# Three up tiles of a feed-forward layer as float32 matmuls ahead of two layer norms

## The reference, cut to what matters

```python
mod = jax.nn.silu(c) @ w_ada[l] + b_ada[l]
sh1, sc1, g1, sh2, sc2, g2 = jnp.split(mod, N_MOD, axis=-1)
...
x = layer_norm(ALPHA * x + g1[:, None] * mix, ln1_g[l], ln1_b[l])

h = layer_norm(x) * (1.0 + sc2[:, None]) + sh2[:, None]
up = causal_dwconv(h @ w_up[l], w_dw_f[l], b_dw_f[l])
v, gt = jnp.split(up, 2, axis=-1)
f = (jax.nn.gelu(gt) * v) @ w_down[l]
x = layer_norm(ALPHA * x + g2[:, None] * f, ln2_g[l], ln2_b[l])
```

## Time and profile before

| what | value |
|---|---|
| median of 3 runs | 1081.65 us (1080.99 to 1084.04) |
| the profiled execution's own time | 1080.48 us |
| its span in the trace | 1078.7 us |
| PE busy | 1042.5 us (97%), 7724 matmuls |
| DVE busy | 775.7 us (72%) |
| ACT busy | 601.7 us (56%) |
| chain that ended last | PE 80%, DVE 12%, ACT 5%, issue 2%, DMA 1% |
| mean granted TensorE clock | 0.992 |

### The profile page before, as it was taken

The page is one execution under the profiler, slowest core; times in us unless marked ns, Lnnn a source line. Parts: engine busy times, 40 slices in busy tenths (PEclk is TensorE's granted clock), DMA queues, the critical chain, the costliest instruction groups (busy, mean ns, idle before and its releaser), DMA issues.

```text
span 1078.7 us, 18838 instructions
## 1 busy us (share of the span) xinstructions
PE 1042.5 (97%) x7724; PEld 982.2 (91%) x7724; DVE 775.7 (72%) x1327; ACT 601.7 (56%) x1029; POOL 1.3 (0%) x13
## 2 busy tenths in 40 slices
PE   7999998999999989989999999999999999999997
PEld 7999998999999988889987899999899878999996
DVE  7989998799877777776667655555789766555555
ACT  5577555666555577552555545544555655545543
POOL 0000000000000000000000000000000000000000
PEclk9999999999999999999999999999999999999999
DMA  9995564477766533441323566566465436565511
GB/s 375 419 363 196 180 237 173 156 251 272 243 194 194 177 98 98 130 145 60 98 79 118 195 196 193 179 194 192 141 212 165 132 116 236 180 191 193 179 60 39
DMA packets 58021, 195.47 MB, mean 181 GB/s; under 512 B 10320, under 2 KB 10704, under 8 KB 57680
## 3 DMA queue, kind: packets, MB, share of 16 engines
q1 hardware_dynamic: 56784, 194.21, 53.5%
q10 hardware_dynamic: 1152, 0.07, 0.1%
HBM read 192.94 MB, written 1.31 MB: 180 GB/s over the span
## 4 chain that ended last, share of the span: by engine, by line
PE 80%; DVE 12%; ACT 5%; issue 2%; DMA 1%; ACTq 0%; POOL 0%; DVEq 0%; POOLq 0%; SPq 0%
PE ps L551 71%; PE ps L848 3%; DVE lo L1740 2%; PE ps L634 2%; DVE B L2152 1%; ACT hi L1158 1%; DVE raw L1727 1%; DVE sm L1917 1%; PE ps L727 1%; DVE xa L1751 0%; DVE B L1808 0%; ACT B L1529 0%; PE ps L707 0%; PE ps L753 0%; ACT L1165 0%
## 5 line engine op out<-in xcount | busy, mean ns | idle before, releaser
L1740 DVE TENSOR_TENSOR lo<-raw,hi 128x1024 fp32r<-128x1024 f32 x311 | 377.7, 1222 | 130.4 <-ACT hi L1158 129.8
L551 PE MATMUL ps<-hh,hi 128*128 128x256 f32 x1568 | 444.2, 283 | 6.8 <-DVE hl L1785 3.2
L551 PE MATMUL ps<-hl,hi 128*128 128x256 f32 x1568 | 439.4, 280 | 0.0
L551 PE MATMUL ps<-hh,lo 128*128 128x256 f32 x1568 | 439.2, 280 | 0.0
L1158 ACT ACTIVATE hi<-raw 128x1024 fp32r<-128x1024 f32 x311 | 324.8, 1052 | 51.0 <-PE ps L551 45.4
L551 PEld LDWEIGHTS ps<-hh,hi 128*128 128x128 f32 x1568 | 296.5, 189 | 10.8 <-DVE lo L1740 3.4
L551 PEld LDWEIGHTS ps<-hl,hi 128*128 128x128 f32 x1568 | 296.5, 189 | 1.6
L551 PEld LDWEIGHTS ps<-hh,lo 128*128 128x128 f32 x1568 | 296.4, 189 | 0.0
L551 PE MATMUL ps<-hi,fh 128*128 128x512 f32 x192 | 76.3, 397 | 0.0
L551 PE MATMUL ps<-lo,fh 128*128 128x512 f32 x192 | 75.9, 395 | 0.0
L551 PE MATMUL ps<-hi,fl 128*128 128x512 f32 x192 | 75.8, 395 | 0.0
(11 more groups left out here) (283 smaller groups left out, 1263.0 us busy)
## 6 DMA issues: line engine op xcount, KB each, us to landing
raw<-in_w SPq DMA_DIRECT2D x359, 512.0 KB, 4.3
B<-in_t SPq DMA_DIRECT2D x2, 512.0 KB, 4.5
xa<-in_x SPq DMA_DIRECT2D x1, 1024.0 KB, 10.1
B<-in_r SPq DMA_DIRECT2D x1, 1024.0 KB, 7.8
out<-h SPq DMA_DIRECT2D x4, 256.0 KB, 2.0
cst<-in_c SPq DMA_DIRECT2D x1, 864.0 KB, 8.4
vec<-in_v SPq DMA_DIRECT2D x1, 328.5 KB, 6.4
ev<-between SPq DMA_DIRECT2D x1, 128.0 KB, 1.9
```

What stands on the lines that cost most here:

```text
L551: m = g.matmul(o, l, r, start=first and n == 0, stop=last and n == 2, skip_group_check=True)
L1740: g.tensor_tensor(lo[:, j % SPLIT, :], raw[:, PLACE[j] % RAW, :], hi[:, j % SPLIT, :].bitcast(F), ALU.subtract).then_inc(*up("lo", j))
```

## The change

The up tiles 0, 22 and 1 (`PLAIN`) are no longer taken from the normalised `h`. They are linear in it, and both norms scale and shift whole tokens. So each tile is taken as eight float32 matmuls of the raw weights with `rx`, the residual ahead of both norms times `ln1_g * (1 + sc2)`, and four more columns are carried behind the 256 tokens (`ln1_g * (1+sc2)`, `ln1_b * (1+sc2)`, `1+sc2`, `sh2`), so that the same matmul gives the four sums of columns that the means and shifts need. Later one matmul with 4 rows (`plain_mend`) adds these sums times four numbers of each token, and DVE multiplies by the token's combined scale, read from a row `rs_row`.

What each engine has more or less:

- PE: no `first_tiles` (72 fp32r matmuls of 256 columns) and no `spin` in the two norms (26); instead 24 float32 matmuls of 260 columns, three small transposes (`plain_sums`), two matmuls and two transposes for the tokens' numbers (`token_rows`), three matmuls of 4 rows (`plain_mend`).
- ACT: no `high` for three units; new are two copies of 8 columns, eight copies into `rx`, some of 2 and 4 columns, a root of 2 columns, three of 4x128, and `tokT` and `rs_row`.
- DVE: no `low` for three units; new are two products of 8 columns, three tiny ones on the tokens' numbers, and three products of 128x256 (`plain_mend`). Both late `ada` rows move ahead of the residual, and two `low` calls move in their place into the norms.
- The convolution of tiles 0, 22 and 1 reads `plain_up` in SBUF, and the banks of PSUM are shared out anew.
- `turn_in` waits for pieces in pairs.

Cut to its core:

```diff
-ROWS_AT = {**{i: 1 for i in range(20, 39)}, 26: 0, 27: 2, 28: 3, 30: 0, 31: 0, 32: 5, 35: 0, 44: 2}
+ROWS_AT = {**{i: 1 for i in range(20, 39)}, 26: 0, 27: 2, 28: 3, 30: 0, 31: 0, 32: 5, 35: 0, 39: 1, 40: 1}
...
+PLAIN = [("up", 0), ("up", FF), ("up", 1)]
+UNITS = [u for u in PLAN if u[0] != "ada" and u not in PLAIN]
...
+            def plain(t, *ks):
+                i = PLAN.index(PLAIN[t])
+                s.wait_ge(*landed(i))
+                s.wait_ge(*at("res", ("x1", 2 * t + 1)))
+                for k in ks:
+                    s.wait_ge(*at("rx", k))
+                    m = g.matmul(bank[UP_BANKS[t]][:, 0:260], raw[:, i % RAW, k * P:k * P + P], rx[:, k, 0:260], start=k == 0,
+                                 stop=k == 7, skip_group_check=True)
...
             turn_in("x1", lambda k: at("res", ("x1", k)))
-            spin(14, 6)
+            plain(0, *range(8))
             turn_out("x1")
-            turn_in("h2", lambda k: at("n_v" if k in X1_V else "n_a", ("x1", k)))
-            spin(12, 6)
-            turn_out("h2")
+            plain(1, 0)
+            turn_in("h2", lambda k: at("n_v" if k in X1_V else "n_a", ("x1", k)),
+                    lambda k: plain(1, 1 + k // 2) if k in (1, 3) else None)
+            plain_sums(0)
+            plain(1, *range(3, 8))
+            plain(2, 0, 1)
+            turn_out("h2", lambda: plain(2, 2))
+            plain_sums(1)
+            plain(2, *range(3, 8))
+            token_rows()
+            plain_mend(0)
+            plain_mend(1)
...
-                first_tiles([(kup, 0), (kup, FF), (kup, 1)], R3, h_of, [free0])
...
+                        if t == 3:
+                            plain_sums(2)
+                            plain_mend(2)
...
+            for k in range(8):
+                s.wait_ge(*at("res", ("x1", k)))
+                s.wait_ge(*at("col_sh"))
+                g.activation(rx[:, k, 0:S], xa[:, k, :], ACT.Copy, scale=rx[:, k, 256:257]).then_inc(*up("rx", k))
             normed("x1")
...
+            plain_sums(0)
+            plain_rows(0)
             normed("h2")
+            plain_sums(1)
+            plain_rows(1)
...
+            def token_rows():
+                s.wait_ge(*at("tokT_mm"))
+                g.activation(tokT, bank[4][0:4, S:2 * S], ACT.Copy).then_inc(*up("tokT"))
+                g.activation(rs_row, bank[4][:, 0:S], ACT.Copy).then_inc(*up("rs_row"))
+
+            turned_high("h2", modcol("sc2"), modcol("sh2"), h, token_rows)
+            plain_sums(2)
+            plain_rows(2)
...
-            for k in range(7):
+            for k in range(5):
                 low(UNIT["out", k] + AHEAD)
...
-            ada(late)
+            low(UNIT["out", 5] + AHEAD)
             normed("h2")
-            ada(late + 1)
+            token_scalars()
+            low(UNIT["out", 6] + AHEAD)
             turned_parts("h2", modcol("sc2"), modcol("sh2"), h)
+            plain_mend(0)
+            plain_mend(1)
             low(UNIT["out", 7] + AHEAD)
```

More of the change, by code:

```diff
@@ L699, in turn_in, with turn_out @@
                         m.then_inc(*up("tok_in", (nid, k // 4)))
-            def turn_out(nid):
+                    if between:
+                        between(k)
+            def turn_out(nid, between=None):
                 for half in range(2):
@@ L706, in turn_out @@
                         for k in range(4 * half, 4 * half + 4):
+                            if k > 5 and nid == "h2":
+                                s.wait_ge(*at("norm_a", (nid, 1)))
                             m = g.transpose(turned_out(nid, k)[:, c * P:c * P + P], nt[:, c, k * P:k * P + P], ident)
+                        if between and not half and not c:
+                            between()
                     m.then_inc(*up("turned", (nid, half)))
+            def plain(t, *ks):
[6 more added lines that the diff above has]
+                                 stop=k == 7, skip_group_check=True)
+                if k == 7:
+                    m.then_inc(*up("plain", t))
@@ new lines, in plain_sums, with plain_mend @@
+            def plain_sums(t):
+                s.wait_ge(*at("wcol", t))
+                g.matmul(bank[UP_BANKS[t]][0:4, 264:392], wcol[:, t, :], ident, is_transpose=True, start=False, stop=True,
+                         skip_group_check=True).then_inc(*up("wrow_mm", t))
+            def plain_mend(t):
+                s.wait_ge(*at("wrow", t))
+                s.wait_ge(*at("tokT"))
+                g.matmul(bank[UP_BANKS[t]][:, 0:S], wrow[:, t, :], tokT, start=False, stop=True,
+                         skip_group_check=True).then_inc(*up("mended", t))
@@ new lines, in token_rows @@
+            def token_rows():
+                s.wait_ge(*at("n_v", ("h2", 1)))
+                s.wait_ge(*at("tok4"))
+                for c in range(2):
+                    m = g.matmul(bank[4][:, c * P:c * P + P], rs_both[:, c, :].to_broadcast([P, P]), ident, start=c == 0,
+                                 stop=True, skip_group_check=True)
+                for c in range(2):
+                    m = g.matmul(bank[4][0:4, S + c * P:S + c * P + P], tok4[:, c, :], ident, is_transpose=True, start=False,
+                                 stop=True, skip_group_check=True)
+                m.then_inc(*up("tokT_mm"))
@@ L1296, in affine, with turned_high @@
                 g.activation(o[:, k, :], turned_out(nid, k), ACT.Identity, scale=gain(k), bias=bias(k)).then_inc(*up("n_a", (nid, k)))
-            def turned_high(nid, gain, bias, o):
+            def turned_high(nid, gain, bias, o, between=None):
                 def high_part(k):
```

105 lines of the change are left out of this document (79 added, 26 removed).

## The result

Over 22 runs of each, the changed kernel takes 1083.64 us (median; 1082.46 to 1086.55) and the kernel before 1080.87 (1077.63 to 1085.65). The ratio is 1.0029, with a 95% interval of 1.0020 to 1.0038: slower by some 3 us, where 1081.2 and "no change" were forecast. The spans of the profiled executions are 1081.1 and 1078.7. A second series, ten runs of the changed kernel against 27 of the one before, gave 1082.28 against 1080.93, ratio 1.0011 (0.9999 to 1.0022): 1.2 to 1.4 us, and an interval that just reaches no change. The loss is real in the first series, small in both, and its size is known only as 1 to 3 us. Kernels of different series are best compared by their ratios to the kernel before, whose median was 1080.56 to 1080.93 in the series of the experiments.

The account below looks back on a forecast made before the run. PE, busy for 97% of the span, was taken as the bound. Tile 2 starting 0.95 us early less a 0.5 us stall gave 0.45 us gained on the median 1081.65: 1081.2 us, range 1078.3 to 1083.6.

Parts of the forecast that it names:

- Out stage: Ahead of the norms: about 0.6 us more DVE work against a 0.47 us pause; cost nothing.
- first norm: Plain tile 0 fills PE's pause and keeps the clock full; turned result 1.35 us early, root not held up by rx.
- weighed rule on a drain: ACT table switch costs 1283 ns plus a drain of about 1380 ns; weighed, but not used in the sum.
- rival 3: A table load holds ACT twice as long where work stands right behind it: 1083.5 us, chance 0.03.
- Second norm: DVE's second statistics lead by 0.7 us, but the lead isn't passed on; ACT starts gain and bias as before.
- rival 2: ACT and DVE take over PE's lead in the second norm, clock full as well: 1078.25 us, chance 0.1.
- Tokens and mending: Behind the second norm PE waits 3.5 us for tokT, one low stretch adds 1.7; tile 2 starts 0.95 us early.
- The start of the sum: Base of the forecast: profiled execution of 1080.48 us and median of 1081.65, from which 0.45 us gain was taken.
- Behind it: After tile 2 starts: one stall of 0.5 us, at low of tile 25; f_lo 0 is in time.
- Rival 1: Clock stays full through the wait for tokT: gain 2.15 us, 1079.5 us, chance 0.2.
- Rival 4: PE pauses 1.7 us or more before 181, low clock with plain matmuls ahead of transposes: 1083.6 us, chance 0.1.
- Rival 5: The wait for tokT eats all that three tiles save; with 1 us more on ACT 1082.2 us, chance 0.07.

Follow-up runs that it names:

- e1: Changed kernel with 22 filler matmuls between token_rows and the first mending matmul, in PE's wait for tokT: 1080.01 us, ratio to before 1.0000.
- e2: Changed kernel with the mending matmuls of up tiles 0 and 1 moved behind the first split tile (23): 1077.93 us, ratio to before 0.9973.
- e9: The kernel before, unchanged, profiled once more: 1081.41 us, ratio 1.0003.
- e7: The kernel before with the narrow matmuls of ba woven into the first three gdn tiles: 1083.69 us, ratio 1.0031.
- e4: The kernel before with its fillers in three norms lengthened (14 to 31, 12 to 26, 14 to 30): 1081.19 us, ratio 1.0002.
- e12: e6 with 28 fillers instead of 14 in the norm of x2: 1076.65 us, ratio to before 0.9959.
- e11: Changed kernel with 11 filler matmuls in PE's wait for tokT, half of e1's: 1081.23 us, ratio to before 1.0007.
- e5: e2 with the narrow matmuls of ba woven into the first three gdn tiles: 1079.77 us, ratio to before 0.9993.
- e10: The changed kernel, unchanged, profiled once more: 1082.28 us, ratio to before 1.0011.
- e6: e2 with ACT's and DVE's weight splits for up tiles 23 and 2 moved ahead: 1075.33 us, ratio to before 0.9952.
- e8: e2 with splits moved ahead, 28 fillers in the norm of x2 and ba woven: 1077.94 us, ratio to before 0.9981.

## Why the prediction was wrong

**Out stage, first norm: right.** Plain tile 0 took 3.67 (3.5 foretold), the eight copies into `rx` 3.30 (3.2), the root followed at 175.74 and held nothing up. Sixteen transposes at the full clock took 2.25, not 1.92, so the low clock cost the first `turn_out` 1.3 us, not 1.6. The table load ended at 171.86 and the dummy began at 171.87, so of the weighed rule on a drain (the Trainium skill, ScalarE: Activation LUTs, "What ACT_TABLE_LOAD costs") this case's trace shows the 1.28 us and no second pause; rival 3 falls.

**Second norm: right.** ACT began gain and bias 16.85 us behind the first `turn_in`, where the kernel before began and where 16.81 was foretold; PE's lead wasn't passed on, as said, so rival 2 falls.

**Tokens and mending: the step that failed.** The wait was 2.88 us (3.5 foretold), ended by the `tokT` copy as said. But "with one low stretch (+1.7)" was wrong: the low clock lasted from 194.0 to 200.9, twice as long as in either norm of the kernel before. The two mends and tile 23 took 7.1 us (193.97 to 201.03) where I had 3.7 at full clock and 5.4 with the stretch; in e1 they take 3.96, so the low clock cost 3.1, not 1.7. I had read the price of a low stretch from two pauses of 1.7 and 2.0 us and used it for one that I expected to be twice as long.

Tile 2 starts 30.68 us behind the first `turn_in` where I had 29.07 (foretold 0.95 under before's 30.02, measured 0.66 over). The difference of 1.6 is 1.4 of low clock, 0.3 for mends that take longer at the full clock than I had, and 0.35 for the third mending with its way through ACT (1.25 against 0.9), less 0.4 because `tokT` came sooner than foretold.

The mechanism was foretold, then, and its price was mis-sized. My sum also had the wait's length nearly right and didn't ask what else PE could do in it; e2 shows that this was worth as much again.

**The start of the sum: a second, smaller error.** My base was one profiled execution and the median of three runs, 1081.65, where 22 runs give 1080.87; against the latter the same sum gives 1080.4. That execution had the low clock in both norms, and the 1.35 us that I booked as PE's gain in the first norm was mostly its removal. e9 and e7 show executions with one low stretch and with none, where `down` 0 is 0.4 and 1.6 us sooner. Against those three, the changed kernel's 36.3 to 36.4 are a loss of 0.7 to 2.4 us. How often each comes was not measured.

So a gain of 0.45 was forecast and a loss of 1.2 to 3.1 measured (by the ratios of the two series). What went wrong up to tile 2 accounts for 1.6 us of that gap and the base for up to 1.6 more; why the first series' loss is so much larger than the second's, no run explains.

**Behind it: about right.** The stall at `low` of tile 25 was 0.13 to 0.3 us (0.5 foretold), `f_lo` 0 made nothing wait, and from `ba` on all executions but the woven ones take 683.6 to 685.0. What the new banks and the pairs in `turn_in` do to the norm of `x2` (0.1 at most foretold) is nothing: e2, with the changed code there, takes 8.60 us from its `turn_in` to `gdn` like before, and 12.00 past `ba` like before.

**The rivals.** Rival 1 (clock full through the wait) was refuted in three executions of three. Rival 4 had the first series' time, 1083.6, by luck: it put the low clock ahead of the transposes, where PE had no pause at all, and the clock was full there. Rival 5 named the place, but priced it as time on ACT.

## What to carry to other kernels

A new wait is priced by its length and by the clock behind it, and the second may be larger: here 2.88 us of waiting were followed by a low clock that cost 3.1 us more. Put first the work that can start piecemeal (a tile that takes its operands as they come) and last the work that needs the one late operand; here that gave 5.9 us up to `down` 0, and a filler in the same wait 3.1. A filler that only holds the clock is worth a try, but only ahead of work that sets the end: in e4 and e12 it gave nothing in the median. And look at a low clock in more than one execution before it is entered in a sum as a gain.

## What was not expected of the hardware

The price of a pause is not one fixed fee: with 2.88, 1.58 and 0.25 us of it ahead of the same matmuls, `down` 0 came at 36.4, 34.9 and 33.3 us. Behind 2.88 us the clock fell in three executions of three, and for 6.8 us. Shorter pauses are a lottery. Between 170 and 420 us the 14 profiled executions have 25 pauses of 1.58 to 2.37 us; 11 were followed by the low clock, 14 were not, and length doesn't sort them:

| pause, us | followed by 0.50 | not followed |
|---|---|---|
| 1.58 to 1.60 | e11 | e2, e5 |
| 1.71 | before | e7 |
| 1.75 to 1.76 (norm of `x2`) | changed, e10, e1 | e2, e5, e6, e11 |
| 1.97 | | e9 |
| 2.03 to 2.05 | before, e9 twice, e7 | before, e7 |
| 2.07 to 2.08 | | e9, e10, e1 |
| 2.35 to 2.37 | e7, e8 | e5 |

The Trainium skill (TensorE: Matmul & The Clock Gate, Part 1, "The HAM clock gate") says that the number of matmuls at the low clock at the start of a kernel varies from run to run. The traces show that variation behind pauses too, and for the changed kernel's longer wait none in three executions.

The clock also falls with PE busy throughout: in the kernel before it goes to 0.50 at 396, when PE has been through the narrow matmuls of `ba` (16 columns each), without any pause. It fell there in all seven executions that had `ba` in one piece and a full clock in the norm of `x2`, and in neither of the two with `ba` woven (e5, e8). Where the clock had already been low in the norm of `x2`, `ba` in one piece was followed by the low clock once (changed) and not three times (e9, e10, e1). What in the narrow matmuls does it wasn't tested.
